# Sparse decode sample by sample, with two page buffers, instead of stage by stage over eight samples

## The reference, cut to what matters

```python
sc = where(causal, index_scores(q_idx, w_idx, kidx_all), -inf)   # per sample: 2048 past keys + the new one
_, sel = lax.top_k(sc, 256)
s = einsum('bqcgd,bqncd->bqcgn', qg, k_sel) * DSA_SCALE + rel_bias[t5_bucket(q_pos - sel)]
p = softmax(where(valid, s, -inf)); o = einsum('bqcgn,bqncd->bqcgd', p, v_sel)
# both groups: RMSNorm, concat, x += gate * (mix @ w_out); then a SwiGLU feed-forward block
```

## Time and profile before

| | us |
|---|---|
| median of 3 runs (1307.5 to 1312.77) | 1309.33 |
| the profiled execution, as timed | 1306.96 |
| its span, first to last instruction | 1305.2 |
| last page's matmuls of the MLA decode end | 673.5 |
| last transpose of the sparse output ends (L1097) | 805.1 |
| output projection begins (L1118) | 815.0 |

### The profile page before, as it was taken

One profiled execution on the slowest core, in us unless ns is written; L12 is line 12 of the kernel. 1 busy time (PEld: TensorE's weight loads), 2 busy tenths in 40 slices (PEclk: granted clock), 3 DMA queues, 4 the chain that ended last, 5 costly groups with the idle time before them and its releaser, 6 DMA issues.

```text
span 1305.2 us, 22152 instructions
## 1 busy us (share of the span) xinstructions
PE 1190.2 (91%) x8993; PEld 1035.9 (79%) x8993; DVE 674.9 (52%) x1449; ACT 396.8 (30%) x766; POOL 91.3 (7%) x135
## 2 busy tenths in 40 slices
PE   6699999978999999999979966976999999979997
PEld 4588885444878999999865345966999999979997
DVE  1635835638897877777651031527333344276330
ACT  3322324523676555555542311012010100100001
POOL 2000002002035000001000010000000000000000
PEclk9799999979999999999987978987999999989999
DMA  9587631022011021113216634221333333332321
GB/s 324 151 268 196 191 114 41 3 70 90 2 74 74 1 74 74 74 74 138 76 65 219 241 141 197 72 58 33 97 88 88 96 89 88 86 89 75 99 72 65
DMA packets 138529, 135.96 MB, mean 104 GB/s; under 512 B 18222, under 2 KB 132283, under 8 KB 135668
## 3 DMA queue, kind: packets, MB, share of 16 engines
q1 hardware_dynamic: 133668, 83.29, 22.0%
q0 software_dynamic: 4784, 51.60, 10.4%
HBM read 131.40 MB, written 3.47 MB: 103 GB/s over the span
## 4 chain that ended last, share of the span: by engine, by line
PE 78%; DVE 11%; DMA 5%; ACT 3%; issue 2%; SPq 1%; POOL 0%; DVEq 0%; ACTq 0%
PE psV L1118 22%; PE psV L943 13%; PE psA L1118 10%; PE psA L686 6%; PE psV L1058 3%; PE psV L880 2%; PE psV L904 2%; PE psA L923 2%; PE psV L642 2%; DMA wide<-cache_kv,rows_of 2%; PE psA L1050 2%; PE psV L748 2%; PE psA L980 2%; PE psV L1089 1%; DVE wide_r L2062 1%
## 5 line engine op out<-in xcount | busy, mean ns | idle before, releaser
L943 PE MATMUL psV<-r_r,wide_r 128*128 128x260 f32 x1536 | 206.4, 288 | 3.6 <-DVE msk L1887 3.2
L943 PEld LDWEIGHTS psV<-r_r,wide_r 128*128 128x128 f32 x1536 | 190.1, 189 | 5.5 <-issue 2.9
L1118 PE MATMUL psV<-qiz_r,wring_r 128*128 128x260 f32 x688 | 124.0, 284 | 0.0
L1409 ACT ACTIVATE wring<-psV 128x512 f32<-128x512 f32 x128 | 76.3, 598 | 86.1 <-PE psV L943 69.7
L1118 PEld LDWEIGHTS psV<-qiz_r,wring_r 128*128 128x128 f32 x688 | 100.5, 190 | 0.0
L1888 DVE TENSOR_REDUCE msk<-wring 128x8 f32<-128x512 f32 x128 | 86.5, 676 | 0.0
L686 PE MATMUL psA<-wide_r,wring_r 128*128 128x260 f32 x432 | 79.7, 289 | 6.6 <-DVE hT_r L2097 6.6
L2051 DVE TENSOR_TENSOR wide<-wide,psV 128x520 f32 (+1 forms) x22 | 15.3, 696 | 134.7 <-PE psV L1118 134.7
L1118 PE MATMUL psA<-qiz_r,r_r 128*128 128x260 f32 x352 | 71.8, 286 | 14.1 <-DVE hT_r L2005 14.1
L1118 PE MATMUL psA<-hT_r,r_r 128*128 128x260 f32 x352 | 71.9, 286 | 0.0
L1118 PE MATMUL psA<-qiz_r,wring_r 128*128 128x260 f32 x352 | 71.4, 285 | 0.0
(11 more groups left out here) (464 smaller groups left out, 2483.3 us busy)
## 6 DMA issues: line engine op xcount, KB each, us to landing
wring<-w_ffn_in SPq DMA_DIRECT2D x44, 512.0 KB, 3.7
wide<-w_ada SPq DMA_DIRECT2D x11, 1024.0 KB, 6.9
wring<-w_ffn_out SPq DMA_DIRECT2D x16, 704.0 KB, 4.7
tok<-w_ada SPq DMA_DIRECT2D x9, 1024.0 KB, 8.1
wring<-w_in SPq DMA_DIRECT2D x24, 256.0 KB, 3.4
wring<-w_out SPq DMA_DIRECT2D x8, 512.0 KB, 4.4
wring<-w_in SPq DMA_DIRECT2D x20, 128.0 KB, 2.7
hT<-x_prompt SPq DMA_DIRECT2D x4, 512.0 KB
```

What stands on the lines that cost most here:

```text
L943: mm = pe.matmul(kx[m % 2][:, hf, :], w, wtab[:, b % 2, l, 2 * k + hf, :], start=(k == 0 and w is high and l == 0), stop=(k == 1 and w is ...
L1118: mm = pe.matmul(out[:, hf, 0:HT], w[:, k, :], x[:, hf * HT:(hf + 1) * HT], start=(k0 + k == 0 and x is xh and w is high), stop=(k0 + k == ...
L1409: A(sq2[m % 2].rearrange("p (x n) -> p x n", x=2), kx[m % 2][:, :, 0:256], ACT.Square).then_inc(kx_squared, 1)
```

## The change

The 64-row stage is gone. The bias is computed once as a table `far` with the keys on the partitions (17 matmuls, `far_table`, in the prompt attention after step 8), and the mask stays on the chip as `maskx`. Every sample then goes through scores, softmax and values by itself, in the layout and by the helpers of the MLA decode. The scores of a key block come from matmuls that hold 128 transposed keys as weights and move the sample's eight query columns (4 for each `k_turn`, 16 for a sample). GpSimd adds mask and bias ahead (`mask_bias`), VectorE adds the scores (`sparse_scores`), and `head_max`, `shift`, `exps`, `row_sums`, `head_sum`, `normalise` run as for MLA, with b from 8 to 15. Sample 0 lies in `qiz`, the others alternate between two buffers (`SLOT`), each fetched once, when the values of the sample two before it are done. On TensorE the values of sample b stand ahead of the keys of sample b+1. `qiz` is free after sample 0, so VectorE splits the prompt's part of the projection's input during samples 1 and 2 (`split_prompt`); only the samples' 64 columns are left for the end. The MLA fold is done per sample inside the pages (`latent_out`, two matmuls after page 10 of the next sample). The first loads of `w_out` start earlier.

The diff, cut to its core:

```diff
+            def far_table():
+                pe.wait_ge(far_loaded, 16)
...
+                for j in range(NPG + 1):
+                    cols = ohf[:, j:PAST:NPG] if j < NPG else ohf[:, PAST:PAST + 1].broadcast_to([NBUCK, 128])
+                    mm = pe.matmul(farps[:, j * 8:(j + 1) * 8], cols, rb64[:, 0:8], start=True, stop=True, skip_group_check=True)
...
+                if u == 8:
+                    far_table()
...
+                if j == 10 and b >= 1:
+                    pe.wait_ge(lat_out, b)
+                    mm = latent_out(b - 1)
                 mm.then_inc(kx_full, 1)
...
             def k_product(b, c4):
-                mm = pe.matmul(sv(n)[0:64, c4 % 2, :], qdz[:, b * 64:(b + 1) * 64], kdT[:, c4 % 2, :], start=(b == 0), stop=(b == 7),
-                               skip_group_check=True)
+                for x in range(4):
+                    j = c4 * 4 + x
+                    mm = pe.matmul(dps[:, j * 8:(j + 1) * 8], kdT[:, c4 % 2, x * 128:(x + 1) * 128], qd[:, b * 8:(b + 1) * 8],
+                                   start=True, stop=True, skip_group_check=True)
...
+            def weigh_values(b):
+                pe.wait_ge(pm_ready, NB + b + 1)
+                pe.wait_ge(lat_out, NB + b)
+                for j in range(NPG + 1):
+                    rows = kvp[SLOT[b]][:, j, 128:256] if j < NPG else tok[:, 4, 416:544]
+                    q = 32 * (j % 4)
+                    mm = pe.matmul(latd[q:q + 32], pm32[b % 2][:, j, :], rows, start=(j < 4), stop=(j > NPG - 4), skip_group_check=True)
+                mm.then_inc(lat_pv, 1)
...
+            k_scores(0)
+            weigh(NB - 1)
+            k_scores(1)
+            pe.wait_ge(lat_out, NB)
+            latent_out(NB - 1).then_inc(ol_full, 1)
+            for b in range(NB):
+                weigh_values(b)
+                if b >= 2:
+                    values_out(b - 1)
+                if b >= 1 and b + 1 < NB:
+                    k_scores(b + 1)
...
+            def sparse_scores(b):
+                par = b % 2
+                v.wait_ge(d_full, b + 1)
+                v.wait_ge(bm_ready, b + 1)
...
+                v.scalar_tensor_tensor(sfull[par][:, 0:NPG].rearrange("p j h -> p (j h)"), dps[:, 0:128], -1.0, bmd[:, par, 0:128],
+                                       ALU.mult, ALU.add).then_inc(d_taken, 1)
...
+            def mask_bias(b):
...
+                if b >= 2:
+                    g.wait_ge(d_taken, b - 1)
+                g.tensor_tensor(bmd[:, b % 2].rearrange("p (j h) -> p j h", h=8), far,
+                                maskx[:, b, :].unsqueeze(2).broadcast_to([128, NPG + 1, 8]), ALU.add).then_inc(bm_ready, 1)
...
+                if b == NB - 3:
+                    for x in range(2):
+                        mask_bias(x)
...
+            for b in range(NB):
+                head_max(NB + b)
+                if b == 0:
+                    g.wait_ge(lat_pv, NB)
+                    kv_rows_of(2, SLOT[2])
+                head_sum(NB + b)
+                if b + 2 < NB:
+                    mask_bias(b + 2)
+                if 3 <= b + 2 < NB:
+                    g.wait_ge(lat_pv, NB + b + 1)
+                    kv_rows_of(b + 2, SLOT[b + 2])
```

More of the change, by code:

```diff
@@ L366, in build @@
         wlow = [wring_r[:, s * 1024:(s + 1) * 1024] for s in range(SPLIT)]
[L367 removed]
+        whigh = [r1_r[:, 5248 + s * 1024:6272 + s * 1024] for s in range(3)] + [wring_r[:, 4096:5120]]
         WD = KF // 2 * 128
@@ L950, in expand, with latent_out @@
                     mm = pe.matmul(last_total[:, 8:16], earlier, ends[:, 8:16], start=True, stop=True, skip_group_check=True)
-                mm.then_inc(kx_full, 1)
+                elif m % 4 == 2 and KA + m // 4 == STEPS + 1:
+                    pe.wait_ge(top_done, 1)
+                    mm = pe.matmul(newm, maskx[:, :, NPG], ident[:, 127:128], start=True, stop=True, skip_group_check=True)
+                if j == 10 and b >= 1:
+                    pe.wait_ge(lat_out, b)
+                    mm = latent_out(b - 1)
+                mm.then_inc(kx_full, 1)
+            def latent_out(b):
+                for k in range(2):
+                    mm = pe.matmul(olps[:, k * 8:(k + 1) * 8], olr[b % 2][:, k * 128:(k + 1) * 128], sel[:, 64:72], start=True, stop=True,
+                                   skip_group_check=True)
+                return mm
             def rope_turn(b):
@@ L1010, in pe_decode @@
                     mix_turn(2 * b + j // 13, b)
-            weigh(NB - 1)
-            n = A_OL
-            pe.wait_ge(a_free, n - 1)
-            pe.wait_ge(lat_out, NB)
-            for k in range(2):
-                for b in range(NB):
-                    c = k * 64 + b * 8
-                    mm = pe.matmul(sa(n)[:, 0, c:c + 8], olb[:, b, k * 128:(k + 1) * 128], sel[:, 64:72], start=True, stop=True,
-                                   skip_group_check=True)
-            mm.then_inc(a_full, 1)
@@ L1021, in pe_decode @@
-            pe.wait_ge(a_free, n + 1)
-            pe.wait_ge(v_free, V_OV - 1)
-            for h in range(H):
-                for k in range(2):
-                    mm = pe.matmul(sv(V_OV)[(h % 2) * 64:(h % 2) * 64 + 64, 0, (h // 2) * 8:(h // 2) * 8 + 8],
-                                   wukv[:, k, h * 128 + 64:(h + 1) * 128], olT[:, k, :].rearrange("p (b h) -> p h b", b=NB)[:, h, :],
-                                   start=(k == 0), stop=(k == 1), skip_group_check=True)
-            mm.then_inc(v_full, 1)
@@ new lines, in k_product, with k_scores @@
+                if c4 == 3:
+                    mm = pe.matmul(dps[0:NB, 128:136], kT[:, SEQ:T], qd[:, b * 8:(b + 1) * 8], start=True, stop=True, skip_group_check=True)
+                    mm.then_inc(d_full, 1)
+            def k_scores(b):
+                for c4 in range(5):
+                    if c4 < 4:
+                        k_turn(b, c4)
+                    if c4 >= 1:
+                        k_product(b, c4 - 1)
+            def weigh_values(b):
[6 more added lines that the diff above has]
+                mm.then_inc(lat_pv, 1)
@@ L1100, in pe_tail @@
+            values_out(NB - 1)
         def pe_tail(pe):
```

285 lines of the change are left out of this document (120 added, 165 removed).

## The result

The changed kernel takes 1366.72 us (median of 4 runs, 1353.14 to 1369.42), against 1311.05 us for the kernel before on the same chip (4 runs, 1307.5 to 1313.14). The ratio is 1.0407, 95% interval 1.0332 to 1.0482. The direction was right; the size was not: +31 us forecast, +55.7 measured, and 1366.7 lies above the range.

What follows compares the result with a forecast made beforehand. TensorE, busy 91% of the span, was taken to bound the kernel, with GpSimd's queue deciding the changed sparse decode. The terms 26.2 + 7.9 - 3.1 = +31.0 us gave 1340.4 us; range 1323 to 1357, 8 in 10 1310 to 1362.

Steps and rivals of the forecast that it cites:

- What bounds the kernel: Whole kernel: TensorE, busy 91% of the span, without gaps in prompt attention and MLA decode; GpSimd's queue expected to decide.
- Ahead of the sparse decode: Prompt attention and MLA pages: table 3.8, clock 0.5, latent_out 3.1, newm 0.5; together 7.9 us more (5 to 11).
- At 1.00 I take half of it, 0.22: Far-bias table in prompt attention: 0.22 us for each of 17 8-column matmuls at clock 1.00, 3.8 us in all.
- The chain pays for that in the attention steps behind the table; between nothing and about 2 us, I take 0.5: Attention behind the table: a fall of TensorE's clock there costs 0.5 us.
- The sparse decode: Sparse samples: GpSimd sets a period of 20.15 us against 15 on TensorE; the stage ends 26.2 us later.
- The passages: GpSimd, sparse decode: changes between reduction and tensor-tensor operation, twice a sample, cost 8.0 and 8.5 us, together 16.5.
- TensorE's own period: Sparse decode on TensorE: keys 9.5, softmax 3.6, values 2.1 and values_out 0.45, given as about 15 us a sample.
- nothing at the passage: Rival, GpSimd in sparse decode: changing operation costs nothing, TensorE sets the period; stage -8.2 us, total 1306; chance 0.09.
- The handover: Sparse output to projection: VectorE has only 64 columns left ahead of the first projection matmul, 3.1 us saved.
- The third: Rival, GpSimd in sparse decode: passage queues behind the fetch, second 15.7 us, period 24.65, total 1363; chance 0.13.
- the short passage: Rival, GpSimd in sparse decode: each change of operation costs 6 us, period 15.65, total 1313; chance 0.09.
- The clock kept at 1.00: Rival, sparse decode: TensorE keeps full clock and GpSimd doesn't wait; period 11.6 us, total 1277; chance 0.03.

## Why the prediction was right in kind and wrong in size

**What bounds the kernel** was read rightly: attention has no gap on TensorE, so every instruction there lengthens the run. GpSimd, 7% busy, set the period of the sparse decode.

**Ahead of the sparse decode** is the step that failed: +7.9 forecast, +37.0 measured. Two sentences of it:

- "At 1.00 I take half of it, 0.22": half of a row at clock 0.50 was taken as if the clock were the only limit. A table's record took 0.22 us at either level (from 343 to 345 us, at 1.00, as from 345 to 347, at 0.50); the contiguous version took 0.11 at 1.00, half of the 0.225 that I had read at 0.50, so the price is right for contiguous weights, and the stride costs the rest: 3.7 us missed. The diff shows the stride (`ohf[:, j:PAST:NPG]`); I read past it.
- "The chain pays for that in the attention steps behind the table; between nothing and about 2 us, I take 0.5": it was 22.7. I had seen that such matmuls let the clock fall and took for granted that attention would win it back at once. The runs show that it need not: the steps behind the table, which had held 1.00 in the earlier trace rows, stayed at 0.50 for 54 us with TensorE covered by records throughout (table alone: +30.6 in all). It isn't that attention can't: its first steps had the clock back within 4 us in the kernel before, and within 7 in the changed one. What decides between 4 and 54 us isn't shown.

Of the remaining 3.0 us at the table's start, 2.2 are there in the run with the table alone as well (340.67 against 338.49), where nothing ahead of it is changed. So they vary from run to run and aren't the change's; the fall of the clock ahead of attention lasted until about 325 us before and until 327 to 328 in both of these. `latent_out` and `newm` in the pages were 3.9 for a forecast of 3.6.

The clock fell with the table in one piece, contiguous or not, and not with the spread matmuls, but TensorE had a record at every moment of the 54 us at 0.50 (348.9 to 402.9): being covered by records didn't hold it up. I had read the same from 16.63 of 17 us at 0.50, for the sparse stage only; in attention it speaks against the change.

**The sparse decode**: +26.2 forecast, +28.7 measured. The passages were 7.1 and 9.8, 16.9 together (forecast 8.0 + 8.5 = 16.5): a right sum of two wrong halves, because I put the fetch's part on neither. The period was 20.7 for 20.15. TensorE's own period, hidden here, is 16.6 in the version with the bias on VectorE, for a forecast of 15: the keys took 10.4 at clock 0.50, within my 9.5 to 10.5, but the sum had the 9.5 and left out the 0.45 of `values_out`. In the changed kernel the clock was at 0.58 in samples 2 to 4, whose keys took about 8 us (771.07 to 779.1 for sample 3), and at 0.50 from there on. The rival "nothing at the passage" had this stage 8.2 us shorter than before; without passages it came out 6.3 shorter (709.8 to 835.1), the longer periods nearly made up for by sample 1, whose values ended 5 us earlier than I had them.

A smaller misreading: the values of five samples wait for a fetch in the kernel before, not of three, for 0.9 to 1.9 us each. No term of the sum hangs on it.

**The handover**: -3.1 forecast, -3.5 measured; from `values_out` to the projection 6.35 us (forecast 6.4).

**The rivals.** The third, the passage queueing behind the fetch, gave 1363, nearest to the measured time, but by the wrong way: its second passage would be 15.7 us and its period 24.65. The profile shows 9.8 and 20.7. A total that fits is no evidence for a mechanism; the milestones are. Nothing at the passage and the short passage are excluded by GpSimd's timeline and by the added idle operation, which alone gave 36.4 us. No run shows the 6 us that the short passage took for both of a sample's passages: the changed kernel has 7.1 and 9.8 in the middle samples, and 9.1 and 5.9 in sample 0. The clock kept at 1.00 is excluded by the granted clock, 0.50 to 0.58 in the middle samples.

**The range** ended at 1362 because the whole miss was in a term that I had given 5 to 11 us. With the measured 37 in it, the forecast would have been 60.1 us above the median, 1369.

## What to carry to other kernels

A short run of thin matmuls in the middle of a dense stretch can cost what it sets off in the clock behind it, not only its own time: here 22.7 us behind 7.5. Don't infer from a stretch that held the clock that it will regain it soon; split such work up between other matmuls (one or two at a time, it left the clock at 1.00 here), and try filling unavoidable TensorE waits with matmuls that nobody needs (12 to 21 us gained here). On GpSimd count the changes between reductions and tensor-tensor operations, not the operations: one of 0.2 us between two reductions cost 6 us of the run each time. Price a matmul's weight load by its stride as well as by its clock (305 against 187 ns here).

## What the hardware showed that I had not expected

- 34 records of 8 columns (3.8 us with contiguous weights, 7.5 with a stride of 64 bytes) took the clock from 1.00 to 0.50, and it stayed there for 37 and 54 us behind them, with TensorE covered by records all the time; after sixteen records of 16 columns ahead of attention it was back within 4 to 7 us.
- A weight load of 32x128 with a stride of 64 bytes took 305 ns against 187, and its pitch of 0.22 us did not change with the clock (343 to 345 us at 1.00, 345 to 347 at 0.50).
- GpSimd's change between reduction and tensor-tensor took 5.7 to 7.5 us without and 9.1 to 11.4 with a 2 MB fetch under way, although its own record of the fetch ends after 1 to 2 us.
- Work that nobody needs made the kernel 12 to 21 us faster, by the medians (18 to 24 matmuls a sample, for a wait of 3.5 us).
